# Six gather buffers instead of eight, and four query-weight blocks of each layer kept in SBUF between two tiles

## The reference, cut to what matters

```python
def block(xb):
    qry = (xb @ w_query).astype(f32).reshape(PEER_BLOCK, PEER_HEADS, 2, PEER_DQ // 2)
    sc = jnp.einsum('thpd,pnd->thpn', qry, sub_keys.astype(f32))
    ...
    act = jax.nn.gelu(jnp.einsum('thed,td->the', u_emb[idx], xb).astype(f32))
    return jnp.einsum('the,thed->td', (gate * act).astype(xb.dtype), v_emb[idx])
```

## Time and profile before

| What | Value |
|---|---|
| Time, median of 3 runs (range) | 1868.19 us (1867.91 to 1868.76) |
| The profiled execution's own time | 1871.29 us |
| Its span, first to last instruction | 1869.2 us |
| Mean DMA rate over the span | 384 GB/s, 717.08 MB |
| Gathers (software queue) | 604.02 MB, 576 issues |
| Weight blocks | 192 issues of 512 KB |
| Busy share: DVE, PE, ACT, POOL | 66%, 64%, 39%, 38% |

### The profile page before, as it was taken

The page is one execution under the profiler, slowest core; times in us unless marked ns, Lnnn a source line. Parts: engine busy times, 40 slices in busy tenths (PEclk is TensorE's granted clock), DMA queues, the critical chain, the costliest instruction groups (busy, mean ns, idle before and its releaser), DMA issues.

```text
span 1869.2 us, 24571 instructions
## 1 busy us (share of the span) xinstructions
PE 1201.5 (64%) x8944; PEld 722.1 (39%) x8944; DVE 1226.2 (66%) x3079; ACT 732.9 (39%) x2000; POOL 701.3 (38%) x651
## 2 busy tenths in 40 slices
PE   8999945565757648865778566656667744444443
PEld 7995812343335326742346144433235400000000
DVE  4642688887765575577674665559765667667664
ACT  2432445434333344284433343247343334333322
POOL 2020144454434333334333434325433354544442
PEclk9999955666878759967789578778767855555555
DMA  5745799999999999999899999999999999999996
GB/s 189 225 136 169 252 421 421 421 391 421 419 420 418 419 391 404 416 419 418 349 419 417 416 418 419 418 422 412 420 419 418 411 418 421 421 421 421 420 422 272
DMA packets 114663, 717.08 MB, mean 384 GB/s; under 512 B 13319, under 2 KB 13447, under 8 KB 40302
## 3 DMA queue, kind: packets, MB, share of 16 engines
q0 software_dynamic: 82944, 604.02, 78.1%
q1 hardware_dynamic: 30590, 110.20, 16.2%
q10 hardware_dynamic: 1008, 1.29, 0.2%
HBM read 711.34 MB, written 4.12 MB: 383 GB/s over the span
## 4 chain that ended last, share of the span: by engine, by line
DMA 49%; PE 25%; DVE 15%; ACT 6%; issue 3%; POOL 1%; SPq 0%; ACTq 0%; POOLq 0%; DVEq 0%
DMA sb_AR<-in_uv,sb_idx 47%; PE PS L1509 9%; DVE sb_AR L1071 7%; PE PS L1774 5%; PE PS L1575 3%; PE PS L1672 2%; DMA sb_W<-in_w 2%; POOL sb_AR L537 1%; ACT sb_DG L605 1%; PE PS L1495 1%; DVE sb_X L1063 1%; ACT sb_gl L602 1%; ACT L602 1%; DVE sb_AR L993 1%; PE PS L1937 1%
## 5 line engine op out<-in xcount | busy, mean ns | idle before, releaser
L537 POOL DMA_INDIRECT sb_AR<-in_uv,sb_idx x576 | 670.1, 1163 | 1017.6 <-PE PS L1774 893.9
L1071 DVE CUSTOM_DVE_ANT_0 sb_AR<-sb_AR 128x1024 f32<-128x1024 f32 x576 | 703.9, 1222 | 465.0 <-DMA sb_AR<-in_uv,sb_idx 464.0
L1774 PE MATMUL PS<-sb_AR,sb_DG 128*32 128x256 f32 x4608 | 497.7, 532 | 551.1 <-ACT sb_DG L605 534.9
L602 ACT ACTIVATE sb_gl<-sb_dots 128x1 f32<-128x1 f32 x576 | 116.3, 202 | 875.5 <-DVE sb_dots L1071 874.0
L1774 PEld LDWEIGHTS PS<-sb_AR,sb_DG 128*32 128x32 f32 x4608 | 120.4, 130 | 869.6 <-ACT sb_DG L605 769.5
L1509 PE MATMUL PS<-sb_hT,sb_W 128*128 128x160 f32 (+1 forms) x2304 | 352.7, 314 | 6.5 <-DMA sb_W<-in_w 5.5
L1509 PEld LDWEIGHTS PS<-sb_hT,sb_W 128*128 128x128 f32 x2304 | 330.5, 212 | 48.0 <-issue 23.8
L605 ACT ACTIVATE sb_DG<-sb_GR,sb_gl 128x32 f32<-128x32 f32 x576 | 185.0, 321 | 18.8
L602 ACT ACT_TABLE_LOAD x66 | 84.7, 1283 | 1.1
L587 ACT ACTIVATE sb_AR<-sb_Hn 32x1024 f32<-32x1024 f32 x72 | 75.8, 1053 | 1.6
L1575 PE MATMUL PS<-sb_W,sb_mixT 128*128 128x512 f32 x128 | 72.0, 690 | 6.2 <-DMA sb_W<-in_w 4.6
(11 more groups left out here) (364 smaller groups left out, 1237.5 us busy)
## 6 DMA issues: line engine op xcount, KB each, us to landing
sb_W<-in_w SPq DMA_DIRECT2D x192, 512.0 KB, 7.9
sb_AR<-in_uv,sb_idx POOLq DMA_INDIRECT x576, 16.6
sb_mixT<-in_kc SPq DMA_DIRECT2D x2, 1024.0 KB, 9.1
sb_hT<-in_vc SPq DMA_DIRECT2D x2, 1024.0 KB, 18.5
out_o_k<-sb_AR SPq DMA_DIRECT2D x1, 1152.0 KB, 11.9
sb_X<-in_x SPq DMA_DIRECT2D x2, 512.0 KB, 7.1
out_o_v<-sb_AR SPq DMA_DIRECT2D x1, 1024.0 KB, 15.6
out_o_y<-sb_Hn SPq DMA_DIRECT2D x2, 512.0 KB, 5.4
```

What stands on the lines that cost most here:

```text
L537: g.indirect_dma_start(UV[:, sl, :], None, T[f"uv{layer}"], bass.IndirectOffsetOnAxis(ap=idx[:, c:c + 1], axis=0)).then_inc(S(f"uv_in{sl}" ...
L602: ch.link(s.activation(gl[:, sl:sl + 1], dots[:, sl:sl + 1], ACT.Gelu_apprx_tanh))
L1071: v.tensor_tensor_reduce(UV[:, sl, 0:D], UV[:, sl, 0:D], Hrep[:, u % 2, :], 1.0, 0.0, ALU.mult, ALU.add, dots[:, sl:sl + 1]).then_inc(S("d ...
L1774: r = mm(PS[32 * q:32 * q + 32, 6 + u % 2, 0:256], DG[:, sl, :], UV[:, sl, o:o + 256], start=(c == 0), stop=(c == 31), skip_group_check=True)
```

## The change

`UVS` goes from 8 to 6, so gather m waits for the matmuls of step m - 6. The two buffers' place (4 x 1024 floats of each partition) becomes `WK`, which holds four weight blocks. SP loads the last four query blocks of a layer into `WK` with one DMA of 2 MB (function `kept`), and they leave the stream: each pass streams 12 query blocks. Layer 0's load is issued in pass 0 behind the first four query blocks of the stream and waits for the residual of pass 0 (`x_mix`); layer 1's is issued behind the first four qkv blocks of pass 2 and waits for the sixteenth query block of pass 1 on PE. PE takes query blocks 12 to 15 of every pass from `WK` and waits for `kept` there. The stream's positions and the counts of `blk` are adapted (`used`, `used_q`). All orders of instructions on DVE, ACT and PE stay as they were, apart from the operands.

```diff
-UVS = 8
+UVS = 6
...
+KEPT = 4
+STREAM = IN_A + IN_B[:-LATE_B] + [B_OUT0 + j for j in OUT_A] + IN_B[-LATE_B:] + list(range(B_OUT0 + 8, B_QKV - KEPT)) \
+    + list(range(B_OUT0, B_QKV - KEPT)) + 2 * list(range(B_QKV, NBLK - KEPT))
...
-S_OUT, S_Q, S_QKV = (48 - LATE_B, 72, 120, 168), (56, 80, 128, 176), (None, None, 96, 144)
+S_OUT, S_Q, S_QKV = (48 - LATE_B, 68, 112, 156), (56, 76, 120, 164), (None, None, 88, 132)
+
+
+def used(i):
+
+
+    return i + 1 + KEPT * sum(i >= s + 16 - KEPT for s in S_Q)
+
+
+def used_q(mp, j):
+    return used(S_Q[mp] + j) if j < 16 - KEPT else used(S_Q[mp] + 15 - KEPT) + j - 15 + KEPT
...
         UV = a(UVS, 2 * D)
+        WK = a(KEPT, D)
...
                     if i >= WSLOTS:
-                        eng.wait_ge(S("blk"), i + 1 - WSLOTS)
+                        eng.wait_ge(S("blk"), used(i - WSLOTS))
...
+            def kept(end):
+                d(WK, T["w"][end - KEPT:end].rearrange("j p f -> p j f")).then_inc(S("kept"), 16)
...
-            stream(S_OUT[0] + 4, S_Q[1] + 4)
+            stream(S_OUT[0] + 4, S_Q[0] + 4)
+            eng.wait_ge(S("x_mix"), 2)
+            kept(B_QKV)
+            stream(S_Q[0] + 4, S_Q[1] + 4)
...
             stream(S_Q[1] + 4, S_QKV[2] + 4)
+            eng.wait_ge(S("blk"), used_q(1, 15))
+            kept(NBLK)
...
-                    block_fm(S_Q[mp] + j, 4 + j % 2, c0, nq)
+                    if j < 16 - KEPT:
+                        block_fm(S_Q[mp] + j, 4 + j % 2, c0, nq)
+                    else:
+                        eng.wait_ge(S("kept"), 16 * (mp // 2 + 1))
+                        for k in range(KT):
+                            r = mm(PS[:, 4 + j % 2, 0:nq], WK[:, j - 16 + KEPT, 128 * k:128 * k + 128],
+                                   hT[:, k, c0:c0 + nq], start=(k == 0), stop=(k == KT - 1))
+                        r.then_inc(S("blk"), 1)
```

More of the change, by code:

```diff
@@ L24 @@
 OUT_A = (4, 5, 6, 7, 0, 1, 2, 3)
-STREAM = IN_A + IN_B[:-LATE_B] + [B_OUT0 + j for j in OUT_A] + IN_B[-LATE_B:] + list(range(B_OUT0 + 8, B_QKV)) \
-    + list(range(B_OUT0, B_QKV)) + 2 * list(range(B_QKV, NBLK))
+KEPT = 4
+STREAM = IN_A + IN_B[:-LATE_B] + [B_OUT0 + j for j in OUT_A] + IN_B[-LATE_B:] + list(range(B_OUT0 + 8, B_QKV - KEPT)) \
+    + list(range(B_OUT0, B_QKV - KEPT)) + 2 * list(range(B_QKV, NBLK - KEPT))
 S_IN_B = [24 + j for j in range(24 - LATE_B)] + [56 - LATE_B + j for j in range(LATE_B)]
 BANK_B = [4 + j % 2 for j in range(24 - LATE_B)] + [2, 3, 5, 2]
-S_OUT, S_Q, S_QKV = (48 - LATE_B, 72, 120, 168), (56, 80, 128, 176), (None, None, 96, 144)
+S_OUT, S_Q, S_QKV = (48 - LATE_B, 68, 112, 156), (56, 76, 120, 164), (None, None, 88, 132)
[3 more added lines that the diff above has]
+    return used(S_Q[mp] + j) if j < 16 - KEPT else used(S_Q[mp] + 15 - KEPT) + j - 15 + KEPT
 C_CW, C_CB, C_AL, C_DT, C_LM, C_GA, C_GX, C_AN, C_CN, C_H0, NCOL = 0, 64, 68, 77, 86, 90, 94, 98, 99, 100, 104
@@ L821, in queries @@
                     upto("q", j)
-                    eng.wait_ge(S("blk"), S_Q[mp] + j + 1)
+                    eng.wait_ge(S("blk"), used_q(mp, j))
                     if j >= 4:
@@ L880, in mixer1 @@
                     upto("qkv", j)
-                    eng.wait_ge(S("blk"), S_QKV[mp] + j + 1)
+                    eng.wait_ge(S("blk"), used(S_QKV[mp] + j))
                     bank = PS[:, j % 4, :]
@@ L1340, in residual @@
                 upto("res")
-                eng.wait_ge(S("blk"), S_OUT[mp] + 8)
+                eng.wait_ge(S("blk"), used(S_OUT[mp] + 7))
                 for t in TILES[mp]:
```

## The result

| | Time, median (range) |
|---|---|
| Kernel before, beside it on the same chip | 1868.47 us (1867.91 to 1869.38, 4 runs) |
| Changed kernel | 1913.6 us (1909.03 to 1921.19, 4 runs) |
| Ratio | 1.0238, 95% interval 1.0221 to 1.0254 |

The account below looks back on a forecast made before the run. DMA was taken to bound the kernel, at 421 GB/s in the quiet stage. Terms -10.0 - 2.3 + 23.2 + 2.8 = +13.7 us on 1868.2 gave 1881.9 us, 0.7% slower; 8-in-10 range 1868 to 1893.

Parts of the forecast that it names:

- What the change saves: Eight fewer weight blocks through DMA: -10.0 us in the query stretches of passes 1 to 3, -2.3 us for layer 0.
- the 2.3 us at the start: Pass 0: layer 0's early load moves four block loads ahead of the first gather; -2.3 us, bounds 0 and -5.0.
- A lone gather of 5.7 us: After a stall of PE, a gather that finds the DMA engines empty lands no faster than 5.7 us after issue.
- the rule built on it: Per PE stall, DMA loses 10.68 - t, at most 4.98 us; t is the first gather's earlier landing time.
- the seven stalls: PE stalls at 395.5, 694.6, 842.2, 921.4, 1041.8, 1300.3 and 1490.3 us; two fewer buffers cost +23.2 us there.
- the three of the earlier trace: Stalls at 492.3, 967.3 and 1334.9 us with weight blocks between gathers; 5.6 us by the rule, counted half, +2.8.
- the halves taken at 921.4 and at the mixed stalls: Half losses: 2.14 us at pass 2's output projection, 2.8 us where weight blocks lie between gathers (492.3, 967.3, 1334.9).
- 1041.8: Stall at the end of pass 2's queries: saving moves the whole stall forward, and a loss of 4.18 us stays.
- Rival 3: Stalls cost more: mixed ones and 921.4 in full, start saving lost, half the 10 us lost; 1894 us, chance 0.13.
- Rival 1: A lone gather takes 4.5 us, so each stall costs 1.2 us less; 1872.4 us, chance 0.13.
- Rival 2: Stalls hidden because the engines stay behind until the next stall; only bytes count, -12.3 us; 1855.9 us, chance 0.08.
- Rival 4: Layer 0's early load delays query block 4 of pass 0 and all gathers by 5.0 us; 1889 us, chance 0.06.

Follow-up runs that it names:

- eight_fewer_bytes: Kernel before, eight buffers; last four query blocks of passes 1 and 3 not loaded, twelfth taken again; 1860.3 us, ratio 0.9946.
- six_alone: Kernel before with six buffers, the two buffers' place empty, all 16 query blocks streamed; 1925.91 us, ratio 1.0289.
- the ladder: Kernel before, stage of steps alone limited to 6, 5, 4, 3, then 2 buffers; 400, 357, 317, 231 GB/s from five down to two.
- before_warm2: Kernel before plus unread PE products, begun as new sums, at four places where PE waits; 1865.12 us, ratio 0.9975.
- before_warm: Kernel before plus six unread PE products behind each head's scores in pass 3 only; 1868.87 us, ratio 0.9987.
- before_warm2b: Kernel before plus unread PE products at four places where PE waits, added in place without new sums; 1865.08 us, ratio 0.9978.

## Why the prediction was wrong

- **What bounds the kernel** was right: DMA, 421 GB/s unchanged in the quiet stage, and a wait of DVE for gathers that grew by 42.4 us, about the whole of the 44.
- **What the change saves**, forecast 12.3 us: measured 10 us (`eight_fewer_bytes`) and 9.5 (`six_alone` against the change). The intervals (3 to 16 and 7 to 13 us) hold 12.3 as well as 10.0, so what came of the 2.3 us at the start can't be told.
- **A lone gather of 5.7 us**: right, 5.5 us at the median of the ladder's last rung and 5.5 to 6.1 behind four stalls.
- **The failed step is the rule built on it**, "the DMA engines then lose 5.7 + 4.98 - t at each stall where this is positive". It lets DMA run at its full rate until the queue is empty. The ladder shows that with five buffers and a landing of 9.8 us the rate is 400 GB/s, with 8.1 us 357. With 9.8 in the place of 5.7 each of the seven stalls of the earlier trace rows takes its full 4.98, in all 34.9, and the three of the earlier trace rows take 9.8 + 7.47 - t = 6.17, 6.47 and 5.17, in all 17.8: 52.7 us, against 54 measured. That is worked out afterwards, with a bound chosen after the result, and near by luck in part, since by stretch it is wrong (4.98 us for the heads of pass 3, which lost 9). The ladder shows the fade in the quiet stage; that it makes the 54 us in the slow stretches is argued from their rates (359, 360, 373 and 367 GB/s in the rows above), not shown by a run of its own.
- **One gather for each stall, and half weights.** The four sharp stalls came out right (17.6 for 16.9 us). In the slow stretches, as I read their rates, every pair of gathers loses, not only the first behind a stall; and the halves taken at 921.4 and at the mixed stalls, because PE would be late or weight loads would use the gap, were not there: 18.4 us measured for the three stretches from 465 to 526 and 869 to 1001, for 4.4 forecast. In full they are 8.8, so the halves are less than a third of that miss.
- **The stalls' length was taken as it was.** The prediction named this as what would make it wrong. In the main they were neither: the 17 long stalls sum to 165.0 us before and 166.0 with six buffers. One grew by 1.3 us behind late rows, and short waits in the heads of pass 3 by 1.2 us each. At 1041.8 the change itself moved the length, against the prediction, which let "the whole stall" move forward: from 17.0 to 11.0 us with the kept blocks, and that is part of how they paid.
- **Rivals.** Rival 3 (more cost, 1894 us) had the direction and one of the reasons, but the saving wasn't halved. Rival 1 fell: no gather came near 4.5 us. Rival 2 did not happen, since DVE waits for DMA more than before. Rival 4's sign showed, at a quarter of its size: PE waits for weights at query block 4 of pass 0, for 1.19 us where the rival had 5 (timeline of PE), and the first gather is issued at 218.0 us, no later than before (220.1). Over the run PE's waits for weights fell (page):

```profile
195.38 2.41 PE L1529 MATMUL PS<-sb_hT,sb_W 128*128 128x160 f32 x16 [1.19 <-DMA sb_W<-in_w]
...
L1529 PE MATMUL PS<-sb_hT,sb_W 128*128 128x160 f32 (+1 forms) x2048 | 312.5, 314 | 2.1 <-DMA sb_W<-in_w 1.2
```

That group waited 5.5 us for weights before (L1509) and waits 1.2 now, all of it at that block.

- **Open** is how the 28 us too many divide. Intervals of PE over 5 us are some 10 us of the 54, by one profile of each kernel; in the rest the fading rate and rows that come late feed each other, and no run holds one fixed.

## What to carry over

The depth of a queue is not to be checked against the latency of one transfer (5.7 us let four buffers seem enough for the quiet stage, where they gave 357 GB/s of 421): measure the rate with 2, 3, 4, 5 and 6 buffers in a quiet stage (one run does it), and take the depth at which it stops rising as the edge. Read GB/s, not the share of busy engines (0.95 stood beside those 357). Where several engines run fixed orders, a late transfer can lengthen a stall (one did, by 1.3 us), but compare the stalls one by one before blaming them: here the long ones kept their length, and the time went between them. And the last buffer before the plateau may still be worth more than the bytes that its place could save: here one was worth 23 us, and its place, filled with weights, 8 (1.0123 against 1.0081, uncertain by as much).

## What was not expected of the hardware

DMA engines counted as busy for 0.95 of the time moved 357 GB/s with four gather buffers (some 2.8 gathers under way, an estimate), and 421 at a share of 1.01 with six or eight. TensorE products into free columns of a PSUM bank cost nothing where PE waits (ratios 0.9978 and 1.0200 for 1 and 1.0238), and hold its clock up (0.81 for 0.67 in the heads, ten transposes in 1.26 for 2.39 us); begun as new sums in a bank in which another one is running, they left a relative error of 0.101 in the outputs (`before_warm2`; none of that kind in `before_warm`), and added in place they left none (`before_warm2b`).
